# Stores of new keys and values during the output projection, another order of the projected heads, and another order of splits and gated units behind two norms

## The reference

```python
x = x + MACARON * gt1 * swiglu(modulate(x, g_ffn1, sh1, sc1), w1_ffn1, w3_ffn1, w2_ffn1)
heads, state = mixer(modulate(x, g_mix, sh2, sc2))
x = x + gt2 * (heads @ w_out)
x = x + MACARON * gt3 * swiglu(modulate(x, g_ffn2, sh3, sc3), w1_ffn2, w3_ffn2, w2_ffn2)

def modulate(x, g, shift, scale):
    return rmsnorm(x, g) * (1.0 + scale) + shift

def project_mix(h, w_in, b_forget, qn_fox, kn_fox, qn_dil, kn_dil):
    z = h @ w_in
    qa, ka, va, fa, qb, kb, vb = jnp.split(z, SPLITS, axis=-1)
    ...                      # q and k of both kinds are normed head by head, 8 heads a kind
    return qa, ka, va, logf, qb, kb, vb
```

## Time and profile before

| | us |
|---|---|
| median of 3 runs | 2530.42 |
| the profiled execution | 2532.02 |
| its span, first to last instruction | 2530.4 |
| stages in its span: norm 1 and the first pairs of mix | about 1034 to 1100 |
| mix with cached keys and values beside it | about 1140 to 1490 |
| steps of prompt attention | about 1490 to 1590 |
| w_out | about 1591 to 1698 |
| norm 2 and the start of FFN 2 | about 1698 to 1740 |

### The profile page before, as it was taken

The page is one execution under the profiler, slowest core; times in us unless marked ns, Lnnn a source line. Parts: engine busy times, 40 slices in busy tenths (PEclk is TensorE's granted clock), DMA queues, the critical chain, the costliest instruction groups (busy, mean ns, idle before and its releaser), DMA issues.

```text
span 2530.4 us, 57187 instructions
## 1 busy us (share of the span) xinstructions
PE 2444.4 (97%) x23159; PEld 2326.6 (92%) x23159; DVE 1190.1 (47%) x1903; ACT 910.4 (36%) x1134; POOL 45.1 (2%) x87
## 2 busy tenths in 40 slices
PE   4899999999999999999999998999999999999999
PEld 4899999999999999999788765998999999999999
DVE  2344444344444446774344434566445444454444
ACT  2332322332223334664244323455333333333332
POOL 0032000000000000000000000000000000000000
PEclk8999999999999999999999999999999999999999
DMA  8988777777887764558899998444444444454444
GB/s 326 395 318 302 284 291 289 293 276 276 300 302 285 282 235 152 211 189 316 313 330 345 360 353 323 173 164 150 166 163 157 171 165 163 158 170 166 165 166 153
DMA packets 140007, 619.52 MB, mean 245 GB/s; under 512 B 17896, under 2 KB 24320, under 8 KB 90736
## 3 DMA queue, kind: packets, MB, share of 16 engines
q1 hardware_dynamic: 135792, 608.54, 65.8%
q0 software_dynamic: 4096, 9.27, 1.0%
HBM read 608.29 MB, written 11.03 MB: 245 GB/s over the span
## 4 chain that ended last, share of the span: by engine, by line
PE 86%; DMA 7%; DVE 2%; SPq 2%; ACT 2%; issue 1%; DVEq 0%; ACTq 0%
PE banks L720 25%; PE banks L721 25%; PE banks L722 24%; PE banks L641 5%; DMA adax<-in_w_ada_dram 2%; DMA raw<-in_w_in_dram 2%; PE banks L909 1%; PE banks L913 1%; SPq L546 1%; DMA kv_y<-in_winv_dram 1%; PE banks L851 1%; DVE w_lo L1385 1%; DMA adaw<-in_w_ada_dram 1%; DMA kv_b<-in_wink_dram 1%; PE banks L688 0%
## 5 line engine op out<-in xcount | busy, mean ns | idle before, releaser
L720 PE MATMUL banks<-h_hi,w_hi 128*128 128x288 f32 x3664 | 1088.5, 297 | 14.1 <-DVE w_lo L1385 9.5
L721 PE MATMUL banks<-h_lo,w_hi 128*128 128x288 f32 x3664 | 1081.9, 295 | 0.0
L722 PE MATMUL banks<-h_hi,w_lo 128*128 128x288 f32 x3664 | 1080.9, 295 | 0.0
L1385 DVE TENSOR_TENSOR w_lo<-raw,w_hi 128x1024 fp32r<-128x1024 f32 (+2 forms) x670 | 764.3, 1182 | 591.0 <-ACT w_hi L1087 589.6
L1087 ACT ACTIVATE w_hi<-raw 128x1024 fp32r<-128x1024 f32 (+2 forms) x670 | 672.1, 1025 | 924.3 <-PE banks L722 521.6
L720 PEld LDWEIGHTS banks<-h_hi,w_hi 128*128 128x128 f32 x3664 | 689.9, 188 | 40.2 <-issue 31.3
L721 PEld LDWEIGHTS banks<-h_lo,w_hi 128*128 128x128 f32 x3664 | 689.9, 188 | 0.6
L722 PEld LDWEIGHTS banks<-h_hi,w_lo 128*128 128x128 f32 x3664 | 689.7, 188 | 0.0
L720 PE MATMUL banks<-g_hi,w_hi 128*128 128x288 f32 x1376 | 409.1, 297 | 0.1
L721 PE MATMUL banks<-g_lo,w_hi 128*128 128x288 f32 x1376 | 406.6, 295 | 0.0
L722 PE MATMUL banks<-g_hi,w_lo 128*128 128x288 f32 x1376 | 406.4, 295 | 0.0
(11 more groups left out here) (250 smaller groups left out, 1198.2 us busy)
## 6 DMA issues: line engine op xcount, KB each, us to landing
raw<-in_w_dram SPq DMA_DIRECT2D x166, 1024.0 KB, 4.8
adaw<-in_w_ada_dram SPq DMA_DIRECT2D x112, 1024.0 KB, 6.7
raw<-in_w_dram SPq DMA_DIRECT2D x64, 896.0 KB, 4.5
raw<-in_w_in_dram SPq DMA_DIRECT2D x49, 1024.0 KB, 8.0
adax<-in_w_ada_dram SPq DMA_DIRECT2D x32, 1024.0 KB, 12.7
raw<-in_w_dram SPq DMA_DIRECT2D x32, 960.0 KB, 4.7
raw<-in_w_out_dram SPq DMA_DIRECT2D x16, 1024.0 KB, 5.0
kv_a<-in_vpool_dram SPq DMA_DIRECT2D x36, 256.0 KB, 4.9
```

Source lines behind the costliest of these rows:

```text
L720: pe.matmul(bank[:, 0:T], hi, m_hi[:, k, :], start=k == 0, stop=False)
L721: pe.matmul(bank[:, 0:T], hi, m_lo[:, k, :], start=False, stop=False)
L722: last = pe.matmul(bank[:, 0:T], lo, m_hi[:, k, :], start=False, stop=k == nk - 1)
L1385: dve.tensor_tensor(w_lo[:, r, a:b], raw[:, r, a:b], w_hi[:, r, a:b].bitcast(F32), ALU.subtract).then_inc(S["lo_ready"], 1)
```

## The change

1. *Places in z.* `PAIR_Z` and `KIND` put the queries of both kinds side by side (`z` 0 to 15) and all keys and values behind them (16 to 47). The order in which w_in's columns are multiplied is the same; `Z_PARTS` maps places back to weight rows. `u_lo` moves out of `z`, over the constants in `big`, and DVE's scratch `u_own` moves from `su` to `tmps`.
2. *Stores.* POOL issues all four stores one behind the other, after the first output rows of w_out are read (`acc_a_read`). `u_hi` no longer lies over a key or value, so ACT and DVE no longer wait for stores ahead of w_out's loop; they wait for them (`heads_stored`, 5 x 16) behind norm 2.
3. *Behind norm 1.* ACT and DVE split tile 6 ahead of the norm of the first pair of heads.
4. *Behind norm 2.* ACT and DVE split tile 4 of FFN 2 first, unit 1 comes ahead of unit 0, and tile 5 is split between them. PE's third pair waits for unit 1 alone.

```diff
-PAIR_Z = (0, 2, 4, 6, 8, 10, 12, 14, 32, 34, 36, 38, 16, 18, 20, 22, 24, 26, 28, 30, 40, 42, 44, 46)
+PAIR_Z = (0, 2, 4, 6, 16, 18, 20, 22, 32, 34, 36, 38, 8, 10, 12, 14, 24, 26, 28, 30, 40, 42, 44, 46)
+Z_PARTS = (0, 2, 1, 3)
...
-        u_lo = (None, h_lo, at("u_lo", [P, KT, T], F32R, mix0 + KT * T * 4))
-        u_own = su[:, 0:2 * TS].rearrange("p (k b s) -> p k b s", k=2, s=NS)
+        u_own = tmps[:, :, :, :]
...
+        u_lo = (None, h_lo, at("u_lo", [P, KT, T], F32R, big0))
...
             pool.dma_start(lf_out, lf[:, :]).then_inc(S["heads_stored"], 16)
-            pool.wait_ge(S["head_ready"], HEADS)
-            store_heads(0, 8)
-            pool.wait_ge(S["acc_b_read"], done(11))
-            store_heads(2, 32)
             pool.wait_ge(S["bias_done"], 2)
             pool.dma_start(selw[:, :], selh).then_inc(S["ld_selw"], 16)
-            pool.wait_ge(S["head_ready"], 2 * HEADS)
-            store_heads(1, 24)
...
-            pool.wait_ge(S["acc_b_read"], done(23))
-            pool.dma_start(kv_out[3], z[:, 40:48, :]).then_inc(S["v_stored"], 16)
+            pool.wait_ge(S["head_ready"], 2 * HEADS)
+            pool.wait_ge(S["acc_a_read"], out.ra + 1)
+            for n, z0 in enumerate((16, 24, 32, 40)):
+                store_heads(n, z0)
...
+                third = seg.norm is not None and isinstance(i, int) and i == 2
-                pe.wait_ge(S["acc_a_read"], 1 if early else seg.ra + i)
+                pe.wait_ge(S["acc_a_read"], 1 if early else seg.ra + (1 if third else i))
...
+            def scaled_first(seg):
+                split_high(seg, 0, 2)
+                act.wait_ge(S["heads_stored"], 5 * 16)
+                unit_silu(seg, 1, acc_a, 0)
+                split_high(seg, 1, 2)
+                act.wait_ge(S["pair_scaled"], 1)
+                unit_silu(seg, 0, scaled_banks[0], 1)
+                unit_silu(seg, 2, acc_a, 2)
...
                 if b == 2:
                     head_squares(0)
-                    split_high(mix, tile_no(b, 1), 0)
+                    split_high(mix, tile_no(2, 1), 0)
+                    split_high(mix, tile_no(3, 0), 0)
                     head_root(0)
                     head_squares(1)
                     continue
...
-                        body(seg, 1, (seg, 0))
+                        split_low(seg, 0, 2)
+                        gated_unit(seg, 1, 0)
+                        split_low(seg, 1, 2)
+                        shift_read(2)
+                        for j in range(2):
+                            scaled(scaled_banks[j][:, 0:T], j).then_inc(S["pair_scaled"], 1)
+                        dve.wait_ge(S["pair_scaled"], 2)
+                        gated_unit(seg, 0, 1)
...
+                if b == 2:
+                    split_low(mix, tile_no(3, 0), 0)
+                    z_copy(2, 0)
+                    head_norm(0)
+                    continue
```

More of the change, by code:

```diff
@@ L396, in run @@
                 chain.end(seg.bodies)
-        KIND = (dict(n=PAGES, q=0, k=8, v=32, new=C_NEW_FOX), dict(n=WT, q=16, k=24, v=40, new=C_NEW_DIL))
+        KIND = (dict(n=PAGES, q=0, k=16, v=32, new=C_NEW_FOX), dict(n=WT, q=8, k=24, v=40, new=C_NEW_DIL))
         SIDES = 2 * GROUPS
@@ L473, in slot @@
                     b = j // 2 if j < FA_TILE else (j - 1) // 2
-                    row = 0 if j == FA_TILE else 1 + PAIR_Z[b] + (j - tile_no(b, 0))
+                    a = PAIR_Z[b] + (j - tile_no(b, 0))
+                    part = a // HEADS
+                    row = 0 if j == FA_TILE else 1 + HEADS * (Z_PARTS[part] if part < 4 else part) + a % HEADS
                     ap = src[row:row + 1, :, :]
@@ L830, in segments @@
                         second_pair(seg, seg.norm)
-                        run(seg, pe, lambda i, seg=seg: pair(seg, i), 2)
+                        pair(seg, 2)
+                        run(seg, pe, lambda i, seg=seg: pair(seg, i), 3)
                     else:
@@ L1179, in body @@
             def body(seg, i):
-                behind = (seg.norm is not None and i in (0, 1) or (seg is out or seg is segs[1]) and i == 0) \
-                    if isinstance(i, int) else False
+                behind = (seg is out or seg is segs[1]) and isinstance(i, int) and i == 0
                 if not behind:
@@ L1186, in body, with unit_silu @@
                 if seg.kind == "up":
[L1187 to L1194, removed]
+                    unit_silu(seg, i, acc_a, i)
+            def unit_silu(seg, i, bank, place):
+                act.wait_ge(S["w_used"], 2 * (seg.n0 + 1) + 4 * i)
+                if not (isinstance(i, int) and seg.up0 + i == 0):
+                    act.wait_ge(S["g_ready"], seg.up0 + place)
+                act.activation(su[:, :], bank[:, 0:T], ACT.Silu).then_inc(S["acc_a_read"], 1)
+            def scaled_first(seg):
[6 more added lines that the diff above has]
+                unit_silu(seg, 2, acc_a, 2)
             def squares_body(seg, i):
@@ L1202, in segments @@
                 for seg in some:
-                    peel = 2 if seg.norm is not None else 1 if seg.squares or seg is segs[1] else 0
-                    for i in range(peel):
-                        body(seg, i)
+                    peel = 3 if seg.norm is not None else 1 if seg.squares or seg is segs[1] else 0
+                    if seg.norm is not None:
+                        scaled_first(seg)
+                    elif peel:
+                        body(seg, 0)
                     if seg.squares:
@@ L1307, in _ @@
                     split_high(mix, FA_TILE, 0)
-                split_high(mix, tile_no(b, 0), 0)
+                if b != 3:
+                    split_high(mix, tile_no(b, 0), 0)
                 if b == 2:
                     head_squares(0)
-                    split_high(mix, tile_no(b, 1), 0)
+                    split_high(mix, tile_no(2, 1), 0)
+                    split_high(mix, tile_no(3, 0), 0)
                     head_root(0)
@@ L1580, in gated_unit @@
                 dve.tensor_tensor(gf[:, :], su[:, :], b[:, 0:T], ALU.mult).then_inc(S["acc_b_read"], 1)
-                dve.wait_ge(S["acc_b_read"], seg.rb + 1 + i)
+                dve.wait_ge(S["acc_b_read"], seg.rb + 1 + place)
                 gh, gl = g_hi[:, bass.ds(i + seg.g0, 1), :], g_lo[:, bass.ds(i + seg.g0, 1), :]
@@ L1628, in segments @@
                         half_gate(8, GROUPS_ADA)
-                    body(seg, 0, late)
+                    if seg.norm is None:
+                        body(seg, 0, late)
                     if seg.ada:
@@ L1868, in _ @@
             modulate(2)
-            shift_read(2)
-            for j in range(2):
-                scaled(scaled_banks[j][:, 0:T], j).then_inc(S["pair_scaled"], 1)
-            dve.wait_ge(S["pair_scaled"], 2)
+            dve.wait_ge(S["heads_stored"], 5 * 16)
             segments(segs[segs.index(out) + 1:])
```

27 lines of the change are left out of this document (12 added, 15 removed).

## The result

The changed kernel takes 2538.16 us (median of 8 runs, 2534.04 to 2541.98), the kernel before 2530.99 in the same session; the ratio is 1.0021, 95% interval 1.0011 to 1.0031. In the first series the medians lie 7.2 us apart, while the ratio makes it 5.3; the text goes by ratios. So the change costs some 3 to 5 us, where the prediction had a gain of 6. The profiled execution took 2538.80 us, span 2537.2.

The account below looks back on a forecast made before the run. PE is busy 97% of the span, so only filling its idle time or bettering its clock helps. Terms -7.3 - 2.2 + 5.0 + 0 = -4.5, with the clock -6.0 against 2530.42, give 2524.4 us, range 2519 to 2530.5.

Parts of the forecast that it names:

- Part 2: w_out: the arriving stores make a weight tile up to 2.6 us late, covered by 3.5 us free: 0.
- the stores hold back w_out: Rival, w_out: POOL's queue is served ahead of SP's, PE stands 7.3 us, time 2531.7; chance 0.07.
- Part 3: Behind norm 1: tile 6 ahead of the root of pair 0 delays tile 7, costing PE +5.0 us.
- Part 1: Mix and attention: with the four stores gone, later loads land sooner and PE's stalls shrink, winning 7.3 us.
- a dip of the clock: Mix, 1220 to 1230: the granted clock of 0.83 costs PE 1.7 us, counted half against the median.
- First store: Mix, store at 1200: stalls of 1.92 and 2.21 near the exponential hang on it; 2.7 us won.
- Second: Mix, store at about 1242: the stall of 1.55 at 1297.53 hangs on a late weight tile; 1.55 us won.
- Third: Store at about 1438: the stall of 1.74 at 1447.91, a wait for cached keys, goes; 1.74 us won.
- Fourth: Store at 1494.51: the stall of 1.32 at 1514.66 goes; 1.32 us won.
- Part 4: Behind norm 2: splitting tile 4 first cuts PE's stall from 3.3 to 1.1, winning 2.2 us.
- the loads not sooner: Rival, mix: SP's own order and waits for free buffers hold the loads, 2.5 of 7.3 won: 2529.5; chance 0.20.
- tile 6 at a cost of 1 us: Rival, behind norm 1: tile 6 lands by 1074, the term of 5.0 falls to at most 1: 2519.9; chance 0.17.

Follow-up runs that it names:

- e9: Changed kernel with the old order behind norm 1, no new wait in FFN 1, and w_out's stores two and two: 2523.19 us, ratio 0.9962.
- e1: Changed kernel with the order behind norm 1 put back, root of the first pair of heads ahead of tile 6: 2529.66 us, ratio 0.9995.
- e4: Changed kernel with the old order behind norm 1, no new wait in FFN 1, and stores a pair of weight tiles apart: 2523.59 us, ratio 0.9962.
- e10: The kernel of e4 measured once more beside the kernel before: 2521.25 us, ratio 0.9958.
- e7: Kernel before with its four stores cut to a few bytes each, new keys and values not stored: 2526.57 us, ratio 0.9973.
- e6: Changed kernel with norm 1's order and the scratch put back, and stores at their old places in mix and attention: 2529.05 us, ratio 0.9983.
- e8: Kernel before with one added instruction, DVE waiting behind part_low for its own last result: 2535.54 us, ratio 1.0008.
- second series: The changed kernel, unaltered, measured again beside the kernel before: 2535.42 us against 2532.78, ratio 1.0010.
- e3: Changed kernel with the four stores in w_out a pair of weight tiles apart instead of in one row: 2530.5 us, ratio 0.9984.
- e2: Changed kernel with DVE's scratch in FFN 1's last loop back in su, without the new wait there: 2532.3 us, ratio 0.9991.

## Why the prediction was wrong, point by point

**The step left out: the wait behind `part_low`.** The prediction told of `u_ready` in the change and gave it no term; the sum has it at nothing by omission. It costs 2.5 us, six waits of PE of 0.42. DVE's timeline, of the kernel before and of the kernel after, at the same point of FFN 1's last loop (the second pair of rows is one round later):

```profile
996.72 0.88 DVE L1423 SCALAR_TENSOR_TENSOR h_lo<-x,par,h_hi  x2
997.51 2.09 DVE L1385 TENSOR_TENSOR w_lo<-raw,w_hi 128x1024 fp32r<-128x1024 f32 x2
```

```profile
1011.76 0.88 DVE L1436 SCALAR_TENSOR_TENSOR h_lo<-x,par,h_hi  x2
1013.05 2.10 DVE L1398 TENSOR_TENSOR w_lo<-raw,w_hi 128x1024 fp32r<-128x1024 f32 x2 [0.41 <-DVE h_lo L1436]
```

Before, the split of weights begins 0.79 us behind the start of `h_lo`, overlapping its end. With the wait it begins 1.29 behind: the overlap is lost and 0.41 us of idle time added. Behind the waiting instruction stands `w_lo`, and PE waits for just that at every pair: of the 0.50 that `w_lo` begins later, 0.42 show on PE. In w_out the same wait costs PE nothing that shows: the stage takes +0.2 to +0.4 in the traces with paced stores, with no stall.

**Part 2, the cover in w_out: the size of the delay failed, not the cover.** The prediction took half of the engines for each queue from the first byte on, from the earlier trace rows, and so a tile up to 2.6 us late against 3.5 of cover. The measured cover is about 4.2; but the tile came 6.7 late (11.8 us from issue to landing, in place of 5.1).

The reading of the earlier trace rows was the first fault. Its 53.8% and 46.8% are means over 5 us, and the store is through before they end. The queues of the kernel before from 1204 to 1207, then from 1208 to 1209 (packets, MB, share of 16 engines):

```profile
q0 software_dynamic: 112, 1.02, 80.8%
q1 hardware_dynamic: 143, 0.26, 22.7%
...
q1 hardware_dynamic: 71, 0.40, 96.8%
q0 software_dynamic: 2, 0.00, 0.1%
```

While the store ran, POOL's queue had four fifths of the engines: 112 packets of 9.1 KB on the mean against SP's 143 of 1.8 KB. So packets went nearly one for one, and the larger ones of POOL tilted the shares to the store, which the prediction took the trace to deny; the row that it held against its rival, the store's queue ahead of SP's, does not speak against it.

POOL's and ACT's timeline of the kernel after, the stores and the split of tile 4:

```profile
1608.85 2.14 POOL L618 DMA_DIRECT2D out_kv_out_dram<-z  x4 [108.25 <-DVE x L1582]
...
1623.23 2.00 ACT L1091 ACTIVATE w_hi<-raw 128x1024 fp32r<-128x1024 f32 x2 [9.27 <-DMA raw<-in_w_out_dram]
```

The transfers of the kernel after: the load of tile 4, issued at 1611.31; the queues (packets, MB, share of 16 engines) from 1611 to 1615.9, in which q0, POOL's, is the only one; and the queues from 1622 to 1626:

```profile
raw<-in_w_out_dram SPq DMA_DIRECT2D x1, 1024.0 KB, 11.8
...
q0 software_dynamic: 209, 1.78, 103.5%
...
q1 hardware_dynamic: 105, 0.85, 50.2%
q0 software_dynamic: 106, 0.83, 49.0%
```

For 4.6 us behind its issue SP's load moves nothing, while POOL's queue has all engines; only then do they share, and evenly. The first packet of the load comes 5.0 us behind its issue, once 2.3 MB, nearly two whole stores, have gone; in the kernel before it comes 1.0 behind. So 4.0 of the 6.7 are this wait, which the prediction put at nothing, and the remaining 2.7 are the sharing that it had at 2.6. "DMA: Bandwidth & Descriptors" of the Trainium skill, section "Queues, rings and completion order", has each engine go round the queues that hold work, a packet at a time: the even rows agree with it (105 packets to 106), the first 4.6 us don't show it. This is the rival "the stores hold back w_out" in part: given 0.07 and 7.3 us, it cost 2.5 of stall and 1.7 of clock (0.83 for 10 us). e9 fits: its two stores go ahead of the load, and it is 4.1 late without harm. The prediction's own upper bound for the step, 7.3, held what came.

**Part 3, tile 6 ahead of the root: right.** Predicted +5.0. In the table it is +5.3 to +5.8 against 0.0 to +2.7 with the old order, means 5.5 and 1.0, so 4.5; by time 5.1 (e1). The two high ones of the old order, e4 and e10 (+2.6 and +2.7), are those whose clock dipped in this stage (0.98 on the mean, 1.00 in the other six); without them the mean is 0.5, and the difference the 5.0 predicted. The mechanism is the one described: tile 6 landed 10.1 us after its issue, the root began at 1085.32, and PE's wait at `head_sums` was 3.71, "near 4", released by DVE's norm of heads. Tile 7 waited 1.11 and not 3: its start is set by its weights, and the clock's dip (0.83 from 1090 to 1100) made tile 6 longer and so the wait shorter. Counted from norm 1's first matmul, tile 7 began 5.6 later than before, where the prediction had 4.9.

**Part 1, the stores leave mix: the sum about right, two of four terms wrong.** Predicted 7.3 and a dip of the clock. By time it is 6.8 (e7) and 5.8 (e6 against e4 and e10). That the sum came near is in part luck: the first place gave more than its term, the second nothing.
- First store: PE gained 3.8 to 5.1 between 1135 and 1233 in the eight traces with the stores moved, and 0.7 on the mean in the three with them in place (2.2 in e7); predicted 2.7 and 1.7 of clock. How much of this is the store's, the traces don't show: e7, without any store, gained no more there than e8 (2.2) with all of them in place, and kept 1.95 of the wait for the exponential.
- Second: nothing. The stall of 1.55 stays in every trace, 1.35 to 3.60, without a store too (e7). The prediction put it to the store because it was the next one behind it; it hangs on a weight tile behind SP's own cached loads.
- Third: 1.9 in all traces with the stores moved or absent, against 0.4 on the mean with them; predicted 1.74.
- Fourth: the stall of 1.32 is gone with the stores moved, but also in e6 and e8 with the stores in place. It was an accident of the one trace; the term should have been near 0.6 (1.45 less the mean of 0, 1.07 and 1.45).

**Part 4, behind norm 2: right, a little small.** Predicted 2.2 and a dip of 1.4. The stall is 1.28 (1.1 predicted), so 2.0 were won, ended by Silu, and the clock 1.00; the table has -3.5 to -3.6 in nine traces with the new order, against -0.1 and -0.2 in the two without. The old order had the dip in each execution that was traced (0.83 in e7 and e8 as well), so all of it was to be counted, not half. The tables of ACT load as the earlier trace rows show: the next instruction follows 0.02 us behind a load of 1.28.

**The sum.** Predicted -6.0. Measured by terms: +2.5 (the wait), +4.5 to 5.1 (part 3), +4.3 (w_out), -5.8 to -6.8 (mix), -3.6 (norm 2), together +1 to +2.5; by time +2.6 and +5.3. The second series lies at the upper end of the terms, the first 3 us above it, and its interval (+2.8 to +7.9) does not reach their middle: what these 3 us are was not settled. What turned the sign are the two zeros, the wait and w_out, 6.8 us. Two prices among the rivals are slightly off by the prediction's own terms, without bearing on its sum: with the loads not sooner 2530.1, not 2529.5, and with tile 6 at a cost of 1 us 2520.4, not 2519.9.

## What to carry to other kernels

Every line of a diff gets a term, a wait that only guards a scratch buffer above all: look what stands behind it on its engine and who waits for that. A stall behind a store is not the store's unless its chain leads to the store; follow the chain first. Transfers that are put in a row behind one another can each be covered and together not: give them the pace of the work that covers them, here one per pair of tiles, and the same bytes cost nothing. A share of the engines is to be read within the transfer: over 5 us, made four fifths look like half.

## What was not expected of the hardware

- A load that SP issued 2.5 us behind POOL's four stores moved nothing for 4.6 us (103.5% of the engines for POOL's queue), where a load issued alone (kernel before) lands in 5.1 us in all. In e9 the same happens with two stores, in e3 with one. What decides that POOL's first two stores go whole ahead, when later ones share 49.0 to 50.2, stays open.
- DVE waiting for its own last result costs 0.41 us of idle time and the overlap with the next instruction.
- Where the clock falls in mix and attention changes from run to run of the same kernel: the changed kernel had 0.66 from 1380 to 1390 in one execution and 0.90 in the other. At one place it is steady: the stall of 2.5 us in w_out left 0.83 over some 10 us in both traces of the changed kernel and in those of e1 and e2.
